# The weight ring of a two-layer diffusion trunk, cut into slots of 512 KB instead of 1 MB

## The reference: what is computed

```
for each group (context, then latent) and each layer:
  sh1,sc1,g1,sh2,sc2,g2 = silu(cond) @ w_mod + b_mod        # 1024 x 6144
  h   = layer_norm(x) * (1 + sc1) + sh1
  a_u,a_v,m_cq,... = split(h @ w_in)                        # 1024 x 3232
  out_a..out_d     = spatial gating, latent attention, neighbourhood and differential attention
  g   = sigmoid(h @ w_gate + b_gate)                        # 1024 x 4096
  mix = (sum of g[b] * (out_b @ w_branch_b)) @ w_out        # 256 or 512 x 1024 each; 1024 x 1024
  x   = layer_norm(alpha x + g1 mix) * ln1_g + ln1_b
  q   = modulate(x, sh2, sc2) @ w_q                         # 1024 x 2048
  s   = q against subkeys; the best 16 of 128 x 128 experts per head, 8 heads
  act = gelu(x . peer_u[expert]) * gate;  ffn = sum of act * peer_v[expert]
  x   = layer_norm(alpha x + g2 ffn) * ln2_g + ln2_b
```

## Time and profile before

| | us |
|---|---|
| median of 3 runs | 3398.67 |
| lowest, highest | 3394.56, 3402.75 |
| the profiled execution | 3404.11 |
| its span in the trace | 3402.3 |

### The profile page before, as it was taken

How to read it: one execution, slowest core, us unless ns; L and a number is a source line. 1 busy time by engine, 2 the same in 40 slices (tenths; PEclk the granted TensorE clock), 3 DMA queues, 4 the chain that set the end, 5 groups by cost and what they waited for, 6 DMA issues and landing times.

```text
span 3402.3 us, 29695 instructions
## 1 busy us (share of the span) xinstructions
PE 2547.6 (75%) x8820; PEld 1464.0 (43%) x8820; DVE 2201.6 (65%) x5396; ACT 711.0 (21%) x1797; POOL 1729.3 (51%) x1540
## 2 busy tenths in 40 slices
PE   7897988979767776577775769788869665667666
PEld 2585645656543223255542224465637222223222
DVE  4534586775679955655449953776764988856665
ACT  1121123441112210033111211244211121111111
POOL 0000274443437764444447763554434577777775
PEclk9898998989879998788887889887989799778988
DMA  7755597877769998878889987887867799999998
GB/s 311 271 202 213 188 370 287 300 278 283 287 244 380 378 369 346 335 273 338 349 342 347 356 313 280 334 312 249 325 252 286 272 348 347 346 355 388 407 414 320
DMA packets 262813, 1070.99 MB, mean 315 GB/s; under 512 B 29824, under 2 KB 30592, under 8 KB 233728
## 3 DMA queue, kind: packets, MB, share of 16 engines
q0 software_dynamic: 221184, 805.40, 63.3%
q1 hardware_dynamic: 38304, 253.14, 19.3%
q10 hardware_dynamic: 3168, 10.55, 0.8%
HBM read 1065.67 MB, written 3.31 MB: 314 GB/s over the span
## 4 chain that ended last, share of the span: by engine, by line
PE 39%; DVE 24%; DMA 14%; POOL 13%; issue 10%; ACT 1%; SPq 0%; DVEq 0%; ACTq 0%; POOLq 0%
PE psum L785 8%; PE psum L696 8%; POOL ring L1658 8%; DMA wring<-in_wpack 7%; PE psum L773 6%; PE psum L944 5%; POOL work L1658 5%; DVE ring L1211 4%; DMA ring<-in_peer_v,experts 4%; DVE work L1308 3%; PE psum L735 2%; PE psum L923 2%; DMA ring<-in_peer_u,experts 2%; DVE work L1211 2%; PE psum L807 1%
## 5 line engine op out<-in xcount | busy, mean ns | idle before, releaser
L696 PE MATMUL psum<-ring,wdiag 128*128 128x512 f32 x1680 | 914.8, 685 | 384.0 <-DMA ring<-in_peer_v,experts 212.3
L1658 POOL DMA_INDIRECT ring<-in_peer_u,experts x488 | 566.6, 1161 | 1003.6 <-DVE dots L1211 462.1
L1658 POOL DMA_INDIRECT ring<-in_peer_v,experts x620 | 685.1, 1105 | 469.1 <-PE psum L696 274.6
L696 PEld LDWEIGHTS psum<-ring,wdiag 128*128 128x128 f32 x1680 | 342.1, 216 | 890.0 <-issue 546.6
L1211 DVE CUSTOM_DVE_ANT_0 work<-work 128x1024 f32<-128x1024 f32 x280 | 338.3, 1224 | 140.4 <-DMA work<-in_peer_u,experts 138.8
L785 PE MATMUL psum<-work,wring 128*128 128x256 f32 (+1 forms) x1760 | 335.4, 351 | 39.9 <-DMA wring<-in_wpack 34.8
L1658 POOL DMA_INDIRECT work<-in_peer_u,experts x280 | 308.2, 1101 | 96.6 <-issue 83.3
L1211 DVE CUSTOM_DVE_ANT_0 ring<-ring,h2a 128x1024 f32<-128x1024 f32 x256 | 304.9, 1221 | 68.8 <-DMA ring<-in_peer_u,experts 68.0
L1211 DVE CUSTOM_DVE_ANT_0 ring<-ring,work 128x1024 f32<-128x1024 f32 x232 | 280.0, 1223 | 96.9 <-DMA ring<-in_peer_u,experts 95.3
L785 PEld LDWEIGHTS psum<-work,wring 128*128 128x128 f32 x1760 | 294.9, 203 | 88.5 <-issue 50.1
L980 ACT ACTIVATE acts<-dots 128x2 f32<-128x2 f32 x384 | 77.7, 203 | 1132.9 <-DVE dots L1211 1089.0
(11 more groups left out here) (201 smaller groups left out, 2922.4 us busy)
## 6 DMA issues: line engine op xcount, KB each, us to landing
wring<-in_wpack SPq DMA_DIRECT2D x175, 1024.0 KB, 8.0
ring<-in_wpack SPq DMA_DIRECT2D x45, 1024.0 KB, 7.1
wring<-in_wpack SPq DMA_DIRECT2D x20, 512.0 KB, 6.7
ring<-in_peer_v,experts POOLq DMA_INDIRECT x620, 6.3
ring<-in_peer_u,experts POOLq DMA_INDIRECT x488, 6.3
work<-in_peer_u,experts POOLq DMA_INDIRECT x280, 6.3
work<-in_rows ACTq DMA_DIRECT2D x4, 1024.0 KB, 11.0
wring<-in_wpack SPq DMA_DIRECT2D x3, 896.0 KB, 9.6
```

The costliest lines, as they stand in the source:

```text
L696: last = nc.tensor.matmul(psum[:, 6 + q, :], wdiag[:, SUM_NO[e] % SMALL, :], row(V_SLOT[e])[:, 512 * q:512 * (q + 1)], start=(e % KSEL == ...
L1658: pool.indirect_dma_start(row(slot), None, a[table], index).then_inc(got[slot], 16)
```

## The change

A slot is half as large, 1024 numbers a row (512 KB), and `wring` has six. It stays 3 MB. In stage m = 0 there are 17 slots (6 + 11 of the gather ring) where there were 8 of double size. The blocks are cut so that a step of TensorE needs one slot:

- `mod`, `in`, `out`: a block of 512 columns comes in four quarters of 256 rows. TensorE goes through them in turn; after each of the first three it counts up `part_used`, and SyncE waits for that count. The mod blocks of VectorE come in quarters, too, with a `w_ready` wait each, but they are freed together by `macc_ready`, as before.
- `gate` and `pq`: one slot for one item, 128 columns with all 1024 rows; it is free when that item is done. The query blocks are computed one by one at their own places, with one accumulation bank each.
- `branch`: one slot for four items (K = 256) or two (K = 512). `small` and `sub` are two slots each.

```diff
-W_SLOT = 4 * 512
-W_RING = 3
+W_SLOT = 1024
+W_RING = 6
...
-    elif _x[0] == "gate" and _x[3] % 4 == 0:
-        SLOTS += [("gate", _m, _x[2], _x[3] // 4, k) for k in range(2)]
+    elif _x[0] == "gate":
+        SLOTS += [("gate", _m, _x[2], _x[3])]
...
-                        if before[0] == "in" and before[3] == 0:
-                            sp.wait_ge(half_used, 7 * before[1] + before[2] + 1)
+                        if before in PART_NO:
+                            sp.wait_ge(part_used, PART_NO[before])
                         elif before[0] == "mod" and mod_by_vector(before[2], before[3]):
                             sp.wait_ge(macc_ready, 8 * before[2] + before[3] - 3)
...
-                        w = [slot(("mod", m, it[3], it[2], k), 4) for k in range(2)]
-                        for k in range(KD):
-                            last = nc.tensor.matmul(out[0:2, :], silu[:, k, :], w[k // 4][:, k % 4, :], start=(k == 0), stop=(k == KD - 1))
-                        last.then_inc(psum_full, 1)
+                        for q in range(4):
+                            w = slot(("mod", m, it[3], it[2], q), 2)
+                            for k in range(2):
+                                kk = 2 * q + k
+                                last = nc.tensor.matmul(out[0:2, :], silu[:, kk, :], w[:, k, :], start=(kk == 0), stop=(kk == KD - 1))
+                            last.then_inc(part_used if q < 3 else psum_full, 1)
...
-                        for half in range(2):
-                            w = slot(("in", m, j, half), 4)
+                        for q in range(4):
+                            w = slot(("in", m, j, q), 2)
...
-                        w = [slot(("gate", m, b, n // 4, k), 4) for k in range(2)]
+                        w = slot(("gate", m, b, n), KD)
...
-                        if c % 4:
-                            continue
-                        outb = [room(("pq", m, c + n)) for n in range(4)]
-                        for kh in range(2):
-                            w = slot(("pq", m, c // 4, kh), 4)
+                        out = room(it)
+                        w = slot(("pq", m, c), KD)
+                        for k in range(KD):
+                            last = nc.tensor.matmul(out[:, 0:N], w[:, k, :], v.hT[:, k, :], start=(k == 0), stop=(k == KD - 1))
+                        last.then_inc(psum_full, 1)
```

136 lines of the change are left out of this document (73 added, 63 removed).

## The result

The changed kernel takes 3293.6 us (median of four executions, 3289.98 to 3303.32), the kernel before 3397.5 (four, 3394.56 to 3402.75): ratio 0.9697, 95% interval 0.9672 to 0.9722, so 104 us less where 61.5 were forecast. The profiled execution took 3296.4 us, its span is 3294.6. Faster was right.

A forecast was written before the change was run, and what follows sets the result against it. It named no single bound; weight flights had 7% of the chain, TensorE's waits for weights 157 us, 126 in m = 2. 4 + 2.5 + 3 + 9 + 28 + 5 + 10 = 61.5 us gave 3337 from 3398.67; range 3295 to 3400.

The forecast's parts named there:

- part 1: Kernel start: first product begins on its first 512 KB, 4 us (0 to 5); a later projection wait, 2.5 us.
- part 2: TensorE's products from mod blocks in m = 2: quarters freed by `part_used`, 3 us (0 to 5).
- The ceiling: DMA in m = 2: 376 GB/s taken as the most that can be had, capping the gains there.
- part 3: Six turns of projection and VectorE's mod product in m = 2: 1.4 us each, 9 us (-8 to 17).
- part 4: Gates, branches, mix and query blocks of m = 2: slots freed singly, 28 us (12 to 38), half clock extra.
- the second window: Last stretch of m = 2, 1700 to 1800 us: 100 us at 352 GB/s become 93.6 at 376.
- The half clock: TensorE's slower products after stalls in m = 2, gone with the waits: 5 us (0 to 12).
- part 5: Latent stages m = 1 and 3: waits for weights at gates shrink, 10 us of 12.5 (0 to 12.5).
- C: Rival: gathers come late and the stretch behind m = 2 takes the gain back, 3380 us; chance 0.18.
- B: Rival: fixed cost per transfer makes turns 3.2 us later, 11.5 us gain in all, 3387 us; chance 0.06.
- A: Rival: weights with smaller packets lose their queue share, 1.4 us more per MB, slower at 3424 us; chance 0.11.
- D: Rival: TensorE's stalls also hold up expert steps and gathers, so more is gained, 3289 us; chance 0.10.

The follow-up runs named there:

- e3: Changed kernel with slots handed back as late as before (gate and query blocks by fours, mod and out quarters at product's end, projection by halves): 3416.2 us, ratio 0.9824.
- e6: Changed kernel, release by quarters kept, but TensorE waits as for large blocks (four mod quarters, two projection or out, four gate or query blocks): 3436.3 us, 0.9881.
- e9: Changed kernel with each quarter of VectorE's mod blocks freed when VectorE is done with it, in layer 1 only: 3275.6 us, ratio 0.9643.
- e11: Kernel before with weight loads of stage m = 2 cut to 16 numbers a row, all waits and releases kept: 3337.2 us.
- e12: Changed kernel with weight loads of stage m = 2 cut to 16 numbers a row: 3278.3 us.
- e5: Changed kernel, unchanged, on another chip: 3382.1 us against 3481.4 for the kernel before there, ratio 0.9735.
- e4: Changed kernel with only gate and query slots freed in fours: 3403.8 us, ratio 0.9807 to the kernel before.
- e14: Changed kernel, fine release kept, but the first of four gates or query blocks waits for all four slots: 3409.9 us, ratio 0.9792.
- e10: Changed kernel with four query blocks computed in one piece at the first one's place, each freed by itself: 3300.7 us, ratio 0.9721.
- e2: Kernel before with each block fetched by two transfers of half the row, ring and waits unchanged: 3509.6 us against 3475.3, ratio 1.0102.
- e13: Changed kernel with mod and out quarters freed at their product's end and projection quarters by halves; gates and query blocks freed singly: 3401.6 us, 0.9787.

## Why the prediction was right and wrong

**Start (part 1): right.** 4 us forecast, first matmul at 9.7 us for 9.6 forecast; the stretch to the end of m = 0 gives 5.9. The 5.0 us wait with 2.5 to win gave 4.3: the whole wait is gone and TensorE is busy for 1.2 us less, but waits for gathers grow by 2.0 there.

**Products from mod blocks (part 2): the step that failed.** 3 us were forecast with 5 as the bound, since the DMA engines were at 0.94 with 376 GB/s. It is 15.5: all 12.2 us of waiting and 3.3 us of TensorE at the lower clock. The ceiling was wrong. These very 43 us run at 412 GB/s with a share of 1.02 (table of windows). The mean had hidden it: cut into 40 slices the stretch before runs above 400 GB/s in 25 of them and falls to 96 and 0 near 1260 us. Nobody asks for anything there: SyncE waits up to 16.1 us at once for TensorE's mod products to give slots back, GpSimd 9.8 us for VectorE. Now there is no such hole. Before (1222 to 1280 us) and after (1204 to 1247):

```profile
GB/s 408 393 399 414 412 415 421 438 410 418 424 435 401 421 415 424 424 427 427 429 435 407 410 415 367 96 0 56 226 435 435 393 263 124 339 316 266 280 331 427
```

```profile
GB/s 353 345 373 416 419 415 423 419 412 412 404 427 419 408 423 419 400 427 423 419 427 419 423 415 404 419 415 427 415 400 404 427 412 419 412 412 423 415 404 408
```

And the transfers did not slow down alike. DMA issues in this stretch, before and then after (count, KB, us to landing):

```profile
wring<-in_wpack SPq DMA_DIRECT2D x8, 1024.0 KB, 8.5
ring<-in_peer_v,experts POOLq DMA_INDIRECT x9, 7.7
```

```profile
wring<-in_wpack SPq DMA_DIRECT2D x16, 512.0 KB, 10.1
ring<-in_peer_v,experts POOLq DMA_INDIRECT x8, 22.9
```

The gathers that fly with them land after 22.9 us where they took 7.7, and TensorE waits for none of them in this stretch. A weight transfer of 512 KB lands after 10.1 us, no sooner than a whole MB did (8.5), so the flights did not get shorter: TensorE begins on the first quarter of a product in place of waiting for all four. A share of 0.94 of the engines said nothing on whether that could be had. The prediction also gave the gain to `part_used`; e3, without it, keeps 46.8 us of this stretch, and e6, with it, loses half.

**Turns (part 3): right in its mechanism, small in size.** Forecast 9 us, bound 17, measured 15.6: 13.4 of waiting, 2.2 by the clock. That `macc_ready` hands back the same 2 MB and so limits the stretch is shown by e9 (16.4 us of waiting in place of 62.0) and from the other side by e11 and e12 (55 us with hardly a byte to load). A turn won 2.2 us of waiting, not 1.4. The flight of a turn's first block was to be under 6 us. In the chain of the changed kernel the six are 6.56, 6.67, 6.24, 3.74, 4.52 and 3.23 us, 5.2 in their mean where it was 6.9, so 1.8 us less; and the 8 records of matmuls behind it take 5.6 us in the mean of the first five turns where they took 6.0, 0.4 less. The two make the 2.2. The second turn:

```profile
1295.94 6.67 DMA wring<-in_wpack
...
1302.66 5.41 PE psum L786 x8
```

TensorE starts on the first 512 KB while the rest lands, as forecast, and e6 (175.0 us where e5 has 163.3) shows that it is this. The term was undersized, not misplaced.

**Gates to query blocks (part 4): right in place and within its bounds, 40.4 us for 33.** Waits went from 38.3 to 2.0 us, 36.3 for a forecast of 28, a cap of 34 and a bound of 38. That the last gates of a half would still wait now and then didn't come true; and the second window, capped at 6.4 us by 376 GB/s, gave 13.3, at 413 GB/s. The half clock was worth 8.9 us in place of 5. The two make 45.2; other waits of TensorE grew by 4.8. By cause the forecast was one-sided, since it saw the release alone: release of gates and query blocks is some 22 us (e4), waiting for each alone is worth as much (28, e14).

**Latent stages (part 5): the second miss.** Forecast 10 us, bound 12.5, the sum of the direct waits. It is 9.9 + 12.2 = 22.1. TensorE's direct waits for weights there were 3.6 and 8.9 us and are gone. With them its waits for VectorE shrank, from 20.8 to 15.2 us and from 28.1 to 21.6: 12.5 + 5.6 + 6.5 = 24.6, about the 22.1. One of them in m = 1, at the gates, the kernel before and then the changed one:

```profile
PE psum L785 <- DVE work L1619: 5.1, 1, 5.1
```

```profile
PE psum L797 <- DVE work L1630: 0.6, 1, 0.6
```

I read it as a knock-on, VectorE late because its gates came late; no run takes it apart. The query blocks' order was costed at nothing, and e10 bears that out, with 442.0 and 322.8 us in the two latent stages. So what failed here is the bound: the direct waits for weights, 12.5 us, were taken as all that these stages could give.

**Given back: 5.4 us** in small pieces (+1.2, +1.3, +1.0, +2.3, -0.4), where the forecast had none.

**The sum.** Parts 2 (12.5 more), 3 (6.6), 4 (7.4), 5 (12.1) and 1 (3.7) are 42.3 us above the forecast, less 5.4 given back: 36.9. With the 9.3 of the tail that is the 46 us by which the trace's span beats it.

**The rivals.** C, that the stretch behind m = 2 takes the gain back, is refuted: 244.2 and 243.8 us. B isn't seen at its price: e2 has 243 transfers more and loses 34 us, 0.14 us for each. The Trainium skill's rule of at least 1 MiB per DMA ("DMA: Bandwidth & Descriptors", Rules for kernel authors) agrees with e2 in sign, 1.0% for half-size transfers alone; as advice for this ring it points the wrong way, since six slots of 512 KB beat three of 1 MB by 3%. Of A it is shown that smaller transfers cost 1% when nothing else is changed, but not that it is by the share of the queue, and its 1.4 us per MB isn't seen in the turns (178.9 us for 178.7); the changed kernel wins three times what e2 loses. D was the nearest with 3289 us, and its reason, that stalls hold up other work, is seen in the latent stages (12 us); 19 us of the extra, though, come from the ceiling (12.5 in part 2, 6.9 in the second window of part 4).

**Open:** what in e2 costs the 34 us, a smaller share of the queue or the issues; what e4 and e13 do together in m1; why C is 326.8 us in e14 and 318.4 in e6, which waits as e14 does and more (one trace each, so some us of a stage aren't settled); how much of the latent stages' extra is knock-on of which engine; what it is worth that a branch block of 512 KB no longer takes a slot of 1 MB, which no run takes apart; and whether the tail's 9.3 us are more than chance.

## What to carry to other kernels

Ask of each ring slot two things apart: how early may the consumer begin on it, and how early does it come back. Here each alone keeps 45 and 59 us of the 99, so one of them cheaply had is half of it, and both must fit the block that returns latest (here VectorE's mod blocks, found by loading almost nothing and seeing which wait stayed). Don't take a mean DMA rate over a long stretch as a ceiling: look at it in slices, for holes in which nothing was asked for (here 0 to 96 GB/s among slices above 400), and look whether what is on the path waits behind what is not.

## What the hardware showed that I had not expected

- DMA moved 412 and 413 GB/s with weights and gathers mixed, share 1.02 to 1.03, and 407 and 414 in slices of 85 us with gathers alone in the kernel before, whose mean over the tail is 377.
- Under that load a weight block lands after 8.9 to 10.1 us, a gather of expert rows in the same stretch after 22.9 to 31.6: most of the delay falls on the gathers. An 8 KB load beside gathers still takes 2.9 to 3.4 us.
- Each half of a block as its own transfer, with nothing else changed, makes the kernel 1.0% slower.
- A product of 8 matmuls (16 records) takes 8.41 us behind a stall of 8.54 us and 7.03 without one; in m = 2 TensorE's busy time falls by 14.5 us for the same work when the stalls go.
- One kernel takes 3397 us on one chip and 3475 to 3481 on others. The difference lies in three stretches with gathers of expert rows; in the tail the best slices run at 407 and 414 GB/s on the one and at 365 and 377 on the other.
